# A two-block transformer kernel: rehearsal matmuls ahead of the products, a signal for each output tile, and a norm moved into the output projection

## What is computed

```python
# first_block, cut
proj = rmsnorm(h, norm_mix_g) @ w_in                 # q, k, v, u
att = chunked_attention(rmsnorm(q), rmsnorm(k), v, rel_bias)      # 512 wide
ssm = s5_mixer(u, ...)                                # 512 wide, ends in y * sigmoid(y @ w_glu + b_glu)
mixed = concatenate([rmsnorm(att, att_out_g), rmsnorm(ssm, ssm_out_g)], axis=-1)
h = h + mixed @ w_out
h = h + memory_attention(rmsnorm(h), rmsnorm(mem), w_q, w_k, w_v, ..., w_o)
h = h + peer_ffn(rmsnorm(h), w_q, keys, u, v)
# second_block, cut
h2 = rmsnorm(x) * (1 + sc1) + sh1; proj = h2 @ w_in   # two attentions, gates
x = x + g1 * ((gate_a * (oa @ w_proj_a) + gate_b * (ob @ w_proj_b)) @ w_out)
x = x + g2 * peer_ffn(rmsnorm(x) * (1 + sc2) + sh2, ...)
```

## Time and profile before

| what | value |
|---|---|
| median of three runs | 3941.26 us |
| profiled execution, own time | 3943.87 us |
| profiled execution, span of the core's instructions | 3942.1 us |
| TensorE busy | 3610.9 us, 92% |
| VectorE busy | 2976.1 us, 75% |
| ScalarE busy | 1705.3 us, 43% |
| mean granted TensorE clock | 0.956 |

### The profile page before, as it was taken

How to read it: one execution, slowest core, us unless ns; L and a number is a source line. 1 busy time by engine, 2 the same in 40 slices (tenths; PEclk the granted TensorE clock), 3 DMA queues, 4 the chain that set the end, 5 groups by cost and what they waited for, 6 DMA issues and landing times. The chain is left out here.

```text
span 3942.1 us, 53935 instructions
## 1 busy us (share of the span) xinstructions
PE 3610.9 (92%) x19130; PEld 3145.5 (80%) x19130; DVE 2976.1 (75%) x6486; ACT 1705.3 (43%) x3194; POOL 742.4 (19%) x523
## 2 busy tenths in 40 slices
PE   7886788999999999999798898869999999999998
PEld 5545576899999988888586666657999999888887
DVE  3654463599888889999677476443998988799998
ACT  3512343233566643333344455223334666533333
POOL 0000000000233344444100000000001433344442
PEclk9968898999999999999898999989999999999999
DMA  3261222355799989999531102112556999899997
GB/s 119 80 227 43 81 91 70 107 163 168 248 306 307 309 332 403 400 401 399 194 101 62 64 9 75 64 60 100 158 162 210 320 308 309 310 405 402 402 399 286
DMA packets 371788, 853.04 MB, mean 216 GB/s; under 512 B 36017, under 2 KB 185137, under 8 KB 368945
## 3 DMA queue, kind: packets, MB, share of 16 engines
q1 hardware_dynamic: 258816, 530.45, 38.6%
q0 software_dynamic: 73728, 268.47, 18.0%
q10 hardware_dynamic: 38976, 50.68, 3.8%
HBM read 753.91 MB, written 94.37 MB: 215 GB/s over the span
## 5 line engine op out<-in xcount | busy, mean ns | idle before, releaser
L1109 POOL DMA_INDIRECT p2f_row<-in_expert_u_rows,p2f_index x128 | 184.2, 1439 | 1387.7 <-POOLq L83 1106.9
L1109 POOL DMA_INDIRECT p1f_row<-in_peer_u_rows,p1f_index x128 | 184.5, 1441 | 1017.9 <-POOLq L83 722.7
L1724 PE MATMUL p1v_out<-p1a_u_hi,p1v_w_hi 128*128 128x512 f32 x768 | 300.1, 391 | 4.3 <-DVE p1v_w_lo L1706 4.3
L1724 PE MATMUL p2v_out<-p2a_u_hi,p2v_w_hi 128*128 128x512 f32 x768 | 299.5, 390 | 4.3 <-DVE p2v_w_lo L1706 4.3
L1724 PE MATMUL p1v_out<-p1a_u_lo,p1v_w_hi 128*128 128x512 f32 x768 | 299.7, 390 | 0.0
L1724 PE MATMUL p1v_out<-p1a_u_hi,p1v_w_lo 128*128 128x512 f32 x768 | 299.7, 390 | 0.0
L1724 PE MATMUL p2v_out<-p2a_u_lo,p2v_w_hi 128*128 128x512 f32 x768 | 299.2, 390 | 0.0
L1724 PE MATMUL p2v_out<-p2a_u_hi,p2v_w_lo 128*128 128x512 f32 x768 | 299.2, 390 | 0.0
L1684 ACT CAST p1a_u_hi<-p1a_u 128x1024 fp32r<-128x1024 f32 x128 | 135.1, 1056 | 276.6 <-PE p1v_out L1724 275.9
L1684 ACT CAST p2a_u_hi<-p2a_u 128x1024 fp32r<-128x1024 f32 x128 | 135.2, 1056 | 257.7 <-PE p2v_out L1724 248.8
L1109 POOL DMA_INDIRECT p2f_row<-in_expert_v,p2f_index x128 | 185.9, 1452 | 237.1 <-DVE p2f_sum L1132 215.1
(11 more groups left out here) (700 smaller groups left out, 10861.3 us busy)
## 6 DMA issues: line engine op xcount, KB each, us to landing
p1a_u<-in_peer_u SPq DMA_DIRECT2D x128, 512.0 KB
p1a_u<-in_peer_v SPq DMA_DIRECT2D x128, 512.0 KB
p2a_u<-in_expert_u SPq DMA_DIRECT2D x128, 512.0 KB
p2a_u<-in_expert_v SPq DMA_DIRECT2D x128, 512.0 KB
gates<-p_kept SPq DMA_DIRECT2D x20, 2048.0 KB, 12.3
acts<-p1a_a ACTq DMA_DIRECT2D x128, 192.0 KB
p1w_a<-acts SPq DMA_DIRECT2D x128, 192.0 KB
acts<-p2a_a ACTq DMA_DIRECT2D x128, 192.0 KB
```

Of the source, the lines that this page charges most:

```text
L1109: self.nc.gpsimd.indirect_dma_start(self.row[:, n % self.RING, :], None, self.u_rows if dot else self.v_rows, bass.IndirectOffsetOnAxis(ap ...
L1724: last = nc.tensor.matmul(out[:, o, :], lhs[:, s, t * P:(t + 1) * P], rhs[:, n % VSLABS, cols], start=(n == 0 and m == 0), stop=(n == KEYS ...
```

## The change

1. **Rehearsal.** At the start of TensorE's list in every `product`, in `queries_keys` and in `peer_values` stand ten matmuls of the 128 x 128 identity with itself, in full precision, into a bank that the first real matmul overwrites.
2. **Tile signals.** In the last slab of the last chunk of a `product` each output tile signals `tile_done`, and `evacuations` of that chunk waits for its own tile.
3. **One tile at a time.** In products without `inside` and with `kt >= SLABS + 4` (wo1, wmo, va, vb, pb, wo2) the earlier chunk is taken one tile ahead of each of the splits `SLABS` to `SLABS + 3`, where before it was taken after all splits.
4. **The norm in wo1.** `feature_norm` is gone. A guest `SsmNorm` does its work in wo1: the squares ahead of ScalarE's casts, the ones matmuls behind slab 0, the root and the four multiplications behind VectorE's split of slab 3; ScalarE's `x_hi` of slabs 4 to 7 waits for `normed`.

```diff
+def rehearse(nc, ident, bank, count=10):
+    for _ in range(count):
+        nc.tensor.matmul(bank[:, 0:P], ident[:], ident[:], start=True, stop=True, skip_group_check=True)
...
+        one_each = not inside and kt >= SLABS + 4
         taken_at = SLABS if inside else kt
+        if first:
+            first.place(tag, sb, sem, out, chunks_out)
+            inside = [first]
...
         @block.tensor
         def _(pe):
+            rehearse(nc, C["ident"], out[:, 0, :])
...
-                    last.then_inc(multiplied, 1)
+                        if c * kt + k == NCH * kt - 1:
+                            last.then_inc(tile_done, 1)
+                    if c * kt + k < NCH * kt - 1:
+                        last.then_inc(multiplied, 1)
...
-            if any(e == which for e, _ in units):
+            if c < NCH - 1 and any(e == which for e, _ in units):
                 eng.wait_ge(multiplied, kt * (c + 1))
...
+                if c == NCH - 1:
+                    eng.wait_ge(tile_done, u + 1)
...
+                    if c >= 1 and one_each and k >= SLABS:
+                        steps = evacuations(act, ON_ACT, c - 1, steps, [k - SLABS])
...
+                    if c == 0 and first:
+                        first.act_source(act, k)
...
+class SsmNorm:
+    def place(self, tag, sb, sem, out, chunks_out):
+        self.sq = sb("sn_sq", [P, 4, SEQ])
+        self.meansq, self.guess, self.tmp = (sb(f"sn_{n}", [P, SEQ]) for n in ("meansq", "guess", "tmp"))
+        self.tot = out[:, 4, :]
+    def act_begin(self, act):
+        for k in range(4):
+            self.nc.scalar.activation(self.sq[:, k, :], self.x[:, k, :], ACT.Square).then_inc(self.squared, 1)
+    def act_source(self, act, k):
+        if k >= 4:
+            act.wait_ge(self.normed, k - 3)
+    def act(self, act, slab):
+        if slab == 3:
+            act.wait_ge(self.mean_ready, 1)
+            self.nc.scalar.activation(self.guess[:], self.meansq[:], ACT.Abs_reciprocal_sqrt).then_inc(
+                self.guess_ready, 1)
+    def pe(self, pe, slab):
+        if slab == 0:
+            pe.wait_ge(self.squared, 4)
+            for k in range(4):
+                last = self.nc.tensor.matmul(self.tot, self.C["ones"][:], self.sq[:, k, :], start=(k == 0), stop=(k == 3),
+                                             skip_group_check=True)
+            last.then_inc(self.totalled, 1)
+    def banks_free(self, pe, slab):
+        if slab == DK:
+            pe.wait_ge(self.mean_ready, 1)
+    def dve(self, dve, slab):
+        if slab != 3:
+            return
+        V = self.nc.vector
+        dve.wait_ge(self.totalled, 1)
+        V.tensor_scalar(self.meansq[:], self.tot, 1.0 / (4 * P), EPS, ALU.mult, ALU.add).then_inc(self.mean_ready, 1)
+        dve.wait_ge(self.guess_ready, 1)
+        refined_rsqrt(V, Chain(dve, self.refined), self.meansq[:], self.guess[:], self.tmp[:], self.tmp[:])
+        for k in range(4):
+            x = self.x[:, k, :]
+            V.scalar_tensor_tensor(x, x, self.gain(k), self.tmp[:], ALU.mult, ALU.mult).then_inc(self.normed, 1)
...
-        feature_norm(nc, "fn2", C, mixT[:, 4:8], 4, mixT[:, 4:8], column(C, "ssm_out_g"))
-        add_product(nc, "wo1", mixT, A["w_out"], h)
+        add_product(nc, "wo1", C, mixT, A["w_out"], h, first=SsmNorm(nc, C, mixT[:, 4:8], column(C, "ssm_out_g")))
...
         @block.tensor
         def _(pe):
+            rehearse(nc, C["ident"], out[:, 0, :])
             for n in range(KEYS):
```

More of the change, by code:

```diff
@@ L120, with product @@
 STRIDED = 2
-def product(nc, tag, srcT, kt, tokens, chunks, SLABS=4, transfers=(), split=None, ahead=None, halves=None, inside=()):
+def rehearse(nc, ident, bank, count=10):
+    for _ in range(count):
+        nc.tensor.matmul(bank[:, 0:P], ident[:], ident[:], start=True, stop=True, skip_group_check=True)
+def product(nc, tag, C, srcT, kt, tokens, chunks, SLABS=4, transfers=(), split=None, ahead=None, halves=None, inside=(), first=None):
     width = max(src.shape[2] for src, _, _ in chunks)
@@ L148, in product @@
         transferred = sem("transferred")
-        x_hi_ready, x_ready, w_hi_ready, w_ready, multiplied = (
-            sem(n) for n in ("x_hi_ready", "x_ready", "w_hi_ready", "w_ready", "multiplied"))
+        x_hi_ready, x_ready, w_hi_ready, w_ready, multiplied, tile_done = (
+            sem(n) for n in ("x_hi_ready", "x_ready", "w_hi_ready", "w_ready", "multiplied", "tile_done"))
         copied = [sem("copied_by_act"), sem("copied_by_dve")]
@@ L224, in _ @@
             steps = 0
+            if first:
+                first.act_begin(act)
             for c, (src, _, _) in enumerate(chunks):
@@ L238, in _ @@
                         guest.act(act, s)
-                if c >= 1 and taken_at == kt:
+                if c >= 1 and taken_at == kt and not one_each:
                     steps = evacuations(act, ON_ACT, c - 1, steps)
@@ L251, in _ @@
                     s = c * kt + k
+                    if c >= 1 and one_each and k >= SLABS:
+                        steps = evacuations(dve, ON_DVE, c - 1, steps, [k - SLABS])
                     if c >= 1 and k == taken_at:
@@ L596, in dve_end @@
         pass
[L599 to L634, removed]
 def attention(nc, tag, C, items, outs, wide, scale, parts=1, lam=None, score_ring=2, turn_ring=2,
@@ L1056, in peer @@
         peer_gates(nc, tag + "g", C, rows, gates, kept, A, W, fetch)
-        peer_values(nc, tag + "v", kept, W, take, fetch)
+        peer_values(nc, tag + "v", C, kept, W, take, fetch)
 class Fetched:
@@ L1144, in gelu, with peer_queries @@
         self.nc.scalar.activation(self.act[:, cols], self.dots[:, cols], ACT.Gelu).then_inc(self.gelu_done, 1)
-def peer_queries(nc, tag, hT, wq, qT, A, keys, keysT, back):
-    product(nc, tag, hT, DK, SEQ,
+def peer_queries(nc, tag, C, hT, wq, qT, A, keys, keysT, back):
+    product(nc, tag, C, hT, DK, SEQ,
             [(wq[c], False, [copy_to(nc, u, qT[:, 4 * c + u, :]) for u in range(4)]) for c in range(HALVES // 4)],
@@ L1633, in _, with peer_values @@
             W.load_gates(sp, 1)
-def peer_values(nc, tag, kept, W, take, fetch):
+def peer_values(nc, tag, C, kept, W, take, fetch):
     A, LOADS, SLABS, G = W.A, W.LOADS, 3, EGROUP
@@ L2345, in block1, with add_product @@
          A["w_peer_q"], A["peer_keys"], A["peer_u"], A["peer_u_rows"], A["peer_v"], A["gates"], A["acts"], AddTo(nc, h))
-def add_product(nc, tag, srcT, w, h):
+def add_product(nc, tag, C, srcT, w, h, first=None):
     def add(dst):
         return ON_DVE, lambda psum: [lambda: nc.vector.tensor_tensor(dst, dst, psum, ALU.add)]
-    product(nc, tag, srcT, DK, SEQ,
-            [(w[half], True, [add(h[:, t, half * BANK:(half + 1) * BANK]) for t in range(TT)]) for half in range(2)])
+    product(nc, tag, C, srcT, DK, SEQ,
+            [(w[half], True, [add(h[:, t, half * BANK:(half + 1) * BANK]) for t in range(TT)]) for half in range(2)],
+            first=first)
 def chunk_attention(nc, C, qkT, v, bias, outT):
@@ L2387, in memory_attention @@
             norm = MemoryNorm(nc, C, A["mem"].rearrange("(t p) d -> p t d", p=P), mem, memT, column(C, "norm_memkv_g"))
-            product(nc, "wmq", hT, DK, SEQ,
+            product(nc, "wmq", C, hT, DK, SEQ,
                     [(A["w_mem_q"][n], True, columns_to(nc, q, n * BANK, BANK, TT)) for n in range(2)], inside=[norm])
@@ L2394, in memory_attention @@
                                  squares=2 * DK + 5, turns=3 * DK + 5, copies=4 * DK, per=3, banks=spare, after=1)
-            product(nc, "wmkv", memT, DK, MEM_LEN,
+            product(nc, "wmkv", C, memT, DK, MEM_LEN,
                     [(A[name][n], True, columns_to(nc, dst, n * BANK, BANK, MT))
@@ L2875, in block2, with value_product @@
          Finish(nc, h, g2, A["out"]))
-def value_product(nc, tag, hT, w, width, dst, transfers=()):
-    product(nc, tag, hT, DK, SEQ, [(w[n], True, columns_to(nc, dst, n * width, width, TT)) for n in range(2)],
+def value_product(nc, tag, C, hT, w, width, dst, transfers=()):
+    product(nc, tag, C, hT, DK, SEQ, [(w[n], True, columns_to(nc, dst, n * width, width, TT)) for n in range(2)],
             SLABS=2, transfers=transfers)
@@ L2958, in add @@
             lambda: nc.vector.tensor_tensor(h[:, t, cols], h[:, t, cols], psum, ALU.add)]
-    product(nc, "wo2", mixT, DK, SEQ, [(w[half], True, [add(t, half) for t in range(TT)]) for half in range(2)],
+    product(nc, "wo2", C, mixT, DK, SEQ, [(w[half], True, [add(t, half) for t in range(TT)]) for half in range(2)],
             SLABS=2)
```

36 lines of the change are left out of this document (23 added, 13 removed).

## The result

The changed kernel took 3897.51 us, the median of four runs (3890.05 to 3903.76), beside 3941.77 us of the kernel before on the same chip (four runs, 3939.38 to 3945.53). The ratio is 0.9886, with a 95% interval from 0.9867 to 0.9905: 44.3 us off, where 47.3 were forecast off the profiled execution and 46 off the median. The profiled execution of the changed kernel was its slowest, 3903.76 us.

A forecast was written before the change was run, and what follows sets the result against it. TensorE was taken as the bound, busy 3610.9 of 3942.1 us, with gains at phase edges and low clock. 11.8 + 14.8 + 20.7 = 47.3 us off 3943.9 gave 3896.6, less 2.6 for the median, say 3895; range 3884 to 3904, chance 0.70.

The forecast's parts named there:

- part 3: Rehearsal at sixteen starts of products and loops: less time at the low clock behind the first matmul, 20.7 us gained.
- Part 1: The norm moved into wo1, its chain covered by slabs 1 to 3: 11.8 us gained, tile signals and rehearsal there included.
- F: The first matmul of a product; in wo1 forecast at 347.5, 4.4 us after the block's first instruction.
- B: A block's first instruction; in wo1 forecast to move from 355.0 to 343.1.
- Part 2: Tile signals and one tile at a time outside wo1: shorter evacuation tails behind the last matmul, 14.8 us gained.
- Group (a): wmkv, qk, va and wo2: clock already low at block start, rehearsal lifts it earlier; 7.5 of 9.0 us regained.
- Group (b): Ten starts with the clock still high at block start; held over a second 2 us gap, 13.2 of 19.8 us regained.
- The argument from the earlier trace: TensorE busy 30 us without pause at 0.50 on 32 of 128 columns; the rehearsal, filling all 128, should lift the clock.

The follow-up runs named there:

- e12_no_one_each: The changed kernel with one_each off: tile signals stay, the earlier chunk is taken after all splits again; 3899.80 us, ratio 0.9908.
- e4_rehearsal_alone: The kernel before with only the rehearsal, without the norm's move, tile signals and one tile at a time; 3920.1 us, ratio 0.9947.
- e5_narrow: The changed kernel with rehearsal matmuls whose stationary operand is 32 columns of the identity instead of 128; 3892.85 us, ratio 0.9872.
- e9_rows64: The changed kernel with rehearsal matmuls of 64 rows and 16 columns in place of 128 and 128; 3916.69 us, ratio 0.9943.

## Why the prediction was right, and where its parts were not

**The time.** 3895 was forecast and 3897.51 measured. That it came so near is in part luck: two errors inside part 3 partly cancel, and most of what they leave was taken back by a loop that the change does not touch. The three parts in the traces, before against after:

- Part 1 was right. From the first square to the end of wo1 it was 64.16 us and is 52.71: 11.45 gained, 11.8 forecast. F came 4.5 us behind B (4.4), the squares were hidden as said, and from F to the last matmul it took 47.47 (47.3). The clock at F was high as forecast, but not by the way meant: the forecast had it low at B and lifted by the rehearsal, and the rehearsal ran at the high level and was held over a gap of 2.0 us.
- Part 2 was right. The tails outside wo1 shrank by 0.6 in wmq, va, vb, p1q and p2q, by 1.74 to 1.79 in wmo, gl and pa, 3.16 in pb and 3.18 in wo2: 14.6, against 14.8. `e12_no_one_each` shows that 6.3 of these need the early chunk.
- Part 3 was right as a sum, 23.5 against 20.7, but not in its terms. I measure each start by the time from its first to its last matmul, which is 24.6 us shorter over the fifteen outside wo1, and take off 1.1 for first matmuls that came later behind their block's start. Group (a) gave 5.3 (7.5 forecast): wmkv, counted with 2.7, gave 0. Its rehearsal ran at the high level, not from a low one as the group supposes, the start was low all the same, and it would have gained nothing at 1.00 either, since VectorE and ScalarE set its pace. Group (b) gave 18.1 of 19.8 (13.2 forecast, a share that no row fixed): six of its ten starts (w1, p1q, gl, pa, pb, p2q) held the clock over a gap of 1.9 to 2.2 us behind the rehearsal. In vb, p1v and p2v there was next to no gap: the first two rehearsed at the low level until then, and p2v's head is short. wmo lost it. wmq, counted at nothing, gave 1.2, of which the rehearsal can hardly be the cause: TensorE idled 5.3 us behind it.

The case that I had weighed against (b), the Trainium skill (TensorE: Matmul & The Clock Gate, HAM oscillation), has bursts of some 2 us fall back each time behind a wait of 3 to 5 us. The start nearest to it is wmq, and it was low: burst 2.47 us, wait 5.3, window 0.75. The gap of 2 us in group (b) is outside what it describes, so my sentence that (b) would give nothing by it asked more of it than it states.

Behind such gaps the clock held in most starts, but not reliably: of nine in the changed kernel (wo1's and wmkv's too) wmo and wmkv fell, and in `e4_rehearsal_alone` wmkv, vb and gl. Over all profiles, 40 rehearsals of ten 128 x 128 matmuls ran wholly at the high level, 2.47 us, with 1.7 to 2.4 us of idleness behind them; 26 held the clock and 14 lost it. The gap's length does not sort them: one of 1.85 us lost it and one of 2.42 kept it. The same start goes either way from run to run (wmkv at 2.02 and at 1.98 us). What decides stays open.

**The argument from the earlier trace rows was wrong.** I put the low clock down to 32 of 128 columns. `e5_narrow` uses 32 columns and works; `e9_rows64` uses the shape that fills most of that stretch, 64 rows x 16 columns, and does not. The conclusion, that a rehearsal of 128 x 128 lifts the clock, was right, but the reason given for it was not.

**Duration of a rehearsal.** 2.2 and 4.5 us were forecast; it took 2.47 at the high level and 3.9 to 4.6 where it began low, and moved the first matmul back by 0.4 in va and 0.8 in p1v.

**Why the profiled execution gained less.** The terms sum to 11.45 + 14.6 + 23.5 = 49.6 us, and the profiled execution is 40.1 shorter. From the end of p2q to p2v's first load it is 655.5 us before and 663.1 after, 7.6 of the missing 9.5, and nothing of the change is in there. Most of it is the gates loop of the second PEER stage. A window over it, of the kernel before and of the changed one:

```profile
3014.00:3404.00 390.00, 388.39 (x2496) 387.77 (x2496) 338.63 (x694) 259.86 (x623) 138.46 (x84) 1.00 0.91 306
```
```profile
2968.00:3365.00 397.00, 391.27 (x2496) 389.27 (x2496) 338.74 (x694) 259.12 (x623) 132.33 (x84) 0.99 0.90 300
```

The same instructions of TensorE take 7 us more, and ScalarE's waits for the loads of its tiles are 7.9 us in the first and 14.3 in the second. From its first to its last matmul the gates loop takes 389 to 397 us in all fourteen profiles, whatever the kernel, and the first stage's loop, which has the same form, 391 to 398. So it is a spread from one execution to the next; that the loads cause it is argued from ScalarE's waits and was not tested. It may also be the source of the 14 us between the fastest and slowest run of the changed kernel, which was only argued too.

## What to carry to other kernels

Where TensorE is the bound, look at the seams between phases: a norm in a phase of its own, the low clock behind idle heads and evacuations in a row behind the last matmul were 44 us of 3942 here, and none of them shows in a busy share. Fill a head with matmuls of a form that a trace has shown to work (here 128 rows with 32 or 128 columns; 64 x 16 did not), right up to the first real one and no further. Check on each start that TensorE is the bound there; where another engine sets the pace, a low clock costs nothing (wmkv). Signal the last chunk by tile, but first clear the engine's backlog of the chunk before. A phase whose chain is shorter than some slabs that do not need it can move behind the first of them, as early as its input allows.

## What the runs showed of the hardware

- The profile's busy share of TensorE does not say whether the clock will rise or hold. Twenty records of 64 rows x 16 columns and of 128 x 32 took the same 2.34 us at the high level; sixteen such rehearsals left 67.0 and 17.6 us at the low level. In the kernel before the clock went from 1.00 to 0.50 within an unbroken row of 64 x 16 matmuls.
- A wait can cost more than its length: 5.43 us of waiting in the middle of wo1 brought 3.5 us at the low level behind it, 7.1 us in all.
- 2.47 us of matmuls at the high level and then 1.7 to 2.4 us of idleness kept the clock in 26 of 40 starts; 5.3 to 5.5 us of idleness kept it in none of five (wmq).
- TensorE began p1v's rehearsal at 1388.16, with the phase's first cast (1388.13) and a microsecond before its first load was issued (1389.16), so a head is to be measured from the first instruction of any engine and not from the first load.
